# Taking the next tiles' output projection, norm and transposes ahead of each tile's gate projection in the conv stage

## What is computed

```python
yp = yp + concat(ya, yb) @ w_out            # layer 0: output projection and residual
h  = rmsnorm(yp, norm_w[1])
qkv, z, a, b = split(h @ w_in_c, C_SIZES)   # 2048 + 1024 + 8 + 8 columns
qkv, conv_new = causal_conv(qkv, prefix, conv_w)   # width 4, depthwise, then SiLU
# later, in the delta stage: o = rmsnorm(o, gdn_norm) * silu(z)
```

## Time and profile before

| | us |
|---|---|
| median of 3 timed runs | 4142.27 |
| lowest and highest of them | 4137.85, 4146.02 |
| profiled execution, span | 4139.1 |
| conv stage in it, first DMA to the last store's issue | 2158.5 to 3367.7 |
| its conv phases begin (group 0, 1, 2, 3) | 2339.98, 2616.00, 2892.43, 3204.17 |

### The profile page before, as it was taken

The page is one execution under the profiler, slowest core; times in us unless marked ns, Lnnn a source line. Parts: engine busy times, 40 slices in busy tenths (PEclk is TensorE's granted clock), DMA queues, the critical chain, the costliest instruction groups (busy, mean ns, idle before and its releaser), DMA issues. The chain is left out here.

```text
span 4139.1 us, 47583 instructions
## 1 busy us (share of the span) xinstructions
PE 3468.1 (84%) x15449; PEld 2016.0 (49%) x15449; DVE 1876.7 (45%) x3884; ACT 1383.0 (33%) x2827; POOL 858.9 (21%) x1709
## 2 busy tenths in 40 slices
PE   7999648999999897786367999989989956997998
PEld 4445324555555555563223444444444534665665
DVE  0000046677777877333810240431511546774674
ACT  1111126656666565640111111111111123442442
POOL 3112253222211110000000000000000006774672
PEclk9999868999999997787688999999989977997999
DMA  7334324544433330003314012011021032223321
GB/s 244 105 96 129 101 76 153 160 141 143 121 112 112 102 94 14 3 3 120 138 47 186 33 44 66 25 56 51 27 65 41 23 112 75 93 93 92 113 82 57
DMA packets 233111, 366.74 MB, mean 89 GB/s; under 512 B 45876, under 2 KB 130909, under 8 KB 228733
## 3 DMA queue, kind: packets, MB, share of 16 engines
q1 hardware_dynamic: 208064, 334.62, 25.2%
q10 hardware_dynamic: 20736, 21.05, 1.5%
q0 software_dynamic: 4096, 8.40, 0.8%
HBM read 279.22 MB, written 106.04 MB: 93 GB/s over the span
## 5 line engine op out<-in xcount | busy, mean ns | idle before, releaser
L1930 PE MATMUL QB<-hT,w_c 128*128 128x512 f32 x1024 | 449.4, 593 | 0.0
L328 PE MATMUL P0A<-w_all,hT 128*128 128x512 f32 (+1 forms) x1200 | 431.7, 521 | 0.0
L631 PE MATMUL PB<-wb,hT_ahead 128*128 128x512 f32 x704 | 366.1, 646 | 3.2 <-ACT prb L751 1.9
L655 PEld LDWEIGHTS PO<-vst,ptT 128*128 128x128 f32 x2176 | 295.4, 207 | 81.5 <-issue 43.6
L655 PE MATMUL PO<-vst,ptT 128*128 128x64 f32 x2176 | 308.7, 287 | 13.4 <-ACT ptT L771 13.2
L328 PEld LDWEIGHTS P0A<-w_all,hT 128*128 128x128 f32 x1200 | 207.5, 191 | 219.6 <-issue 219.6
L1930 PEld LDWEIGHTS QB<-hT,w_c 128*128 128x128 f32 x1024 | 190.0, 190 | 217.1 <-issue 217.1
L1875 PE MATMUL QS<-w_o,yT 128*128 128x512 f32 x544 | 274.6, 669 | 17.4 <-ACT yT L2043 17.4
L642 PE MATMUL PT<-ident,sm 128*128 128x128 f32 x1088 | 198.8, 308 | 106.0 <-ACT sm L763 105.8
L1899 PE MATMUL QA<-w_c,hT 128*128 128x512 f32 (+1 forms) x768 | 254.8, 488 | 5.7 <-ACT hT L2059 5.7
L771 ACT COPY ptT<-PT 128x512 f32<-128x512 f32 (+3 forms) x320 | 164.9, 518 | 275.1 <-PE PT L642 274.1
(11 more groups left out here) (412 smaller groups left out, 5317.7 us busy)
## 6 DMA issues: line engine op xcount, KB each, us to landing
wb<-in_w_in_ab SPq DMA_DIRECT2D x176, 512.0 KB, 3.7
out_c_all<-crow SPq DMA_DIRECT2D x256, 64.0 KB, 1.6
w_all<-in_w_in_ab SPq DMA_DIRECT2D x48, 256.0 KB, 8.1
out_pr_all<-pr_out SPq DMA_DIRECT2D x17, 546.0 KB, 2.9
pra<-out_pr_all SPq DMA_DIRECT2D x16, 546.0 KB, 4.6
x_rows<-in_x_all SPq DMA_DIRECT2D x17, 512.0 KB, 5.5
yab<-out_yab_all SPq DMA_DIRECT2D x17, 512.0 KB, 3.6
xin<-in_x_all SPq DMA_DIRECT2D x17, 512.0 KB, 4.2
```

The source lines that it names most:

```text
L328: ins = pe.matmul(PA[u % 6][:, 0:b - a], hT[:, t % (LAG + 2), c, :], w_all[:, c, a:b], start=(c == 0), stop=(c == KD - 1))
L631: ins = pe.matmul(PB[:, :], hT[:, 2 * q + k, :], wb[:, u % 4, k, :], start=(q == 0 and k == 0), stop=(q == 3 and k == 1))
L655: ins = pe.matmul(PO[:, h * HD:(h + 1) * HD], ptT[:, v % 2, k * P:(k + 1) * P], vst[:, 4 * c + k, a * HD:(a + 1) * HD], start=(c == 0 and ...
L1930: ins = pe.matmul(PB[b % 2][:, 0:N], w_c[:, c, b * P:(b + 1) * P], hT[:, c, 0:N], start=(c == 0), stop=(c == KD - 1))
```

## The change

On all engines the steps of a tile are put in another order, and the work runs further ahead. Ahead of `z_proj(T)` now stand, as one piece `ahead(T)`: `turn_h(T)`, the matmuls of `out_proj(T+1)`, and the transposes of `yab` for tile T+2 (`turn_y(T+2)`). `turn_h` writes to the banks `PB`, which hold nothing outside the conv blocks, in place of `PT`. ACT's `sub_front` is split into `turned_y` (the copies to `yT`) and `normed`; its order becomes `sub_back(T)`, `normed(T+1)`, `turned_y(T+2)`, then the gate's tanh of T. At the end of each of the first three groups the piece for the next group's first tile is run too: on PE between the matmuls of block 15 and the transposes of block 14, on the others behind the blocks. SP's loads and stores are cut and ordered to match. The first pieces stand in front of the loop, and in the last group (5 tiles) `left` shortens them. No arithmetic and no transfer is added or removed.

```diff
 sync:
+            def rows_in(T):
+                sp.wait_ge(S["yT_ps"], after(2 * T))
+                sp.dma_start(yab[:, :], io["yab_all"][ds(T * P, P), :]).then_inc(S["yab2_loaded"], 16)
+
+            def x_in(T):
+                sp.wait_ge(S["y1_ready"], after(2 * T))
+                sp.dma_start(xin[:, :], io["x_all"][ds(T * P, P), :]).then_inc(S["x2_loaded"], 16)
...
+            def ahead(T, left):
+                if left >= 1:
+                    sub_out(T + 1)
+                if left >= 2:
+                    x_in(T + 2)
+                if left >= 3:
+                    rows_in(T + 3)
+
             def group(G, n):
-                for s in range(n + 1):
-                    if s < n:
-                        if s < GT:
-                            next_in(G * GT + s)
-                        sub_out(G * GT + s)
+                for s in range(n):
+                    T = G * GT + s
                     if s:
-                        z_out(G * GT + s - 1)
+                        ahead(T, n - 1 - s if n > GT else 3)
+                    z_out(T)
                 blocks(G, n > GT)
+                if n == GT:
+                    ahead(G * GT + GT, 3)
 tensor:
-            def out_proj(T):
-
+            def turn_y(T):
                 pe.wait_ge(S["yab2_loaded"], after(16 * (T + 1)))
-                pe.wait_ge(S["hT2_sb"], after(2 * T))
+                pe.wait_ge(S["yT_sb"], after(2 * T))
...
+            def out_proj(T):
                 pe.wait_ge(S["yT_sb"], after(2 * T + 2))
                 pe.wait_ge(S["y1_ready"], after(2 * T))
...
             def turn_h(T, s):
                 pe.wait_ge(S["hn2_ready"], after(T + 1))
-                pe.wait_ge(S["yT_sb"], after(2 * T + 2))
+                pe.wait_ge(S["hT2_sb"], after(2 * T))
...
-                        ins = pe.transpose(PT[u][:, k * P:(k + 1) * P], hn[:, c * P:(c + 1) * P], ident[:, :])
+                        ins = pe.transpose(PB[u][:, k * P:(k + 1) * P], hn[:, c * P:(c + 1) * P], ident[:, :])
...
-            def z_proj(T, s):
+            def z_proj(T, s, G):
                 pe.wait_ge(S["hT2_sb"], after(2 * T + 2))
+                if s == 0:
+                    pe.wait_ge(S["crow_ready"], after(G * NBLK))
...
+                    if b == NBLK and not sample:
+                        pe.wait_ge(S["raw_ready"], after((G + 1) * NBLK))
+                        ahead(G * GT + GT, 0, 3)
...
+            def ahead(T, s, left):
+
+                turn_h(T, s)
+                if left >= 1:
+                    out_proj(T + 1)
+                if left >= 2:
+                    turn_y(T + 2)
+
             def group(G, n):
-                for s in range(n + 1):
+                for s in range(n):
                     T = G * GT + s
-                    if s < n:
-                        out_proj(T)
                     if s:
-                        z_proj(T - 1, s - 1)
-                    if s < n:
-                        if s == 0:
-                            pe.wait_ge(S["crow_ready"], after(G * NBLK))
-                        turn_h(T, s)
+                        ahead(T, s, n - 1 - s if n > GT else 3)
+                    z_proj(T, s, G)
                 blocks(G, n)
...
+            turn_y(0)
+            out_proj(0)
+            turn_y(1)
+            ahead(0, 0, 3)
             with pe.Fori(0, GROUPS - 1) as G:
 scalar:
+            def ahead(T, s, left):
+
+                sub_back(T, s)
+                if left >= 1:
+                    normed(T + 1)
+                if left >= 2:
+                    turned_y(T + 2)
...
                     if s:
-                        z_gate(T - 1, G)
-                    if s < n:
-                        sub_back(T, s)
+                        ahead(T, s, n - 1 - s if n > GT else 3)
+                    z_gate(T, G)
                 blocks(G, n)
...
+                if n == GT:
+                    ahead(G * GT + GT, 0, 3)
 vector:
             def group(G, n):
-                for s in range(n + 1):
-                    if s < n:
-                        residual(G * GT + s)
-                    if s:
-                        z_gate(G * GT + s - 1)
+                for s in range(n):
+                    T = G * GT + s
+                    if s and (n == GT or s < n - 1):
+                        residual(T + 1)
+                    z_gate(T)
                 blocks(G, n)
+                if n == GT:
+                    residual(G * GT + GT + 1)
```

More of the change, by code:

```diff
@@ L1833, in blocks @@
                           .then_inc(S["s_stored%d" % (b % 2)], 16)
-            def group(G, n):
-                for s in range(n + 1):
-                    if s < n:
-                        if s < GT:
-                            next_in(G * GT + s)
-                        sub_out(G * GT + s)
+            def ahead(T, left):
[5 more added lines that the diff above has]
+                    rows_in(T + 3)
+            def group(G, n):
+                for s in range(n):
+                    T = G * GT + s
                     if s:
-                        z_out(G * GT + s - 1)
+                        ahead(T, n - 1 - s if n > GT else 3)
+                    z_out(T)
                 blocks(G, n > GT)
+                if n == GT:
+                    ahead(G * GT + GT, 3)
             sp.dma_start(crw[0:DB * 3, :], io["state_conv"]).then_inc(S["pre_loaded"], 16)
+            rows_in(1)
+            sub_out(0)
+            x_in(1)
+            rows_in(2)
+            ahead(0, 3)
             with sp.Fori(0, GROUPS - 1) as G:
@@ L2027, in tanh_and_rows, with turned_y @@
                 act.activation(cvt[:, 0:N], cva[:, b % 2, 0:N], ACT.Tanh).then_inc(S["cvt_ready"], 1)
+            def ahead(T, s, left):
[4 more added lines that the diff above has]
+                    turned_y(T + 2)
             def group(G, n):
[L2030 removed]
+                for s in range(n):
                     T = G * GT + s
[L2032 to L2033 removed]
                     if s:
[L2035 to L2037 removed]
+                        ahead(T, s, n - 1 - s if n > GT else 3)
+                    z_gate(T, G)
                 blocks(G, n)
[L2040 removed]
+                if n == GT:
+                    ahead(G * GT + GT, 0, 3)
+            def turned_y(T):
                 for u in range(2):
@@ L2044, in sub_front, with normed @@
                        .then_inc(S["yT_sb"], 1)
+            def normed(T):
                 act.wait_ge(S["y1_ready"], after(2 * T + 2))
@@ L2058, in sub_back @@
                         h = hT[:, c, s * P:(s + 1) * P] if s < GT else hT_s[:, c, :]
-                        ins = act.activation(h, PT[u][:, k * P:(k + 1) * P], ACT.Copy, scale=nw1[:, c:c + 1])
+                        ins = act.activation(h, PB[u][:, k * P:(k + 1) * P], ACT.Copy, scale=nw1[:, c:c + 1])
                     ins.then_inc(S["hT2_sb"], 1)
@@ L2068, in _ @@
             act.wait_ge(S["c2_loaded"], after(16 * 4))
+            turned_y(0)
+            normed(0)
+            turned_y(1)
+            ahead(0, 0, 3)
             with act.Fori(0, GROUPS - 1) as G:
@@ L2201, in _ @@
             dve.wait_ge(S["pre_ready"], after(1))
+            residual(0)
+            residual(1)
             with dve.Fori(0, GROUPS - 1) as G:
```

## The result

The changed kernel takes 4017.16 us in the median of 4 runs (4012.09 to 4030.71), against 4140.06 for the kernel before in its 4 runs (4133.15 to 4146.02). The ratio is 0.9708, 95% interval 0.9688 to 0.9727: 123 us less. The forecast of 4026 was 9 us too high, and the time lies inside the stated range.

What follows compares the result with a forecast made beforehand. PE bounds the conv stage, with some 35 us a group lost to waits and slow clock. Gains of 3.5 + 31.9 + 32.3 + 48.8 = 116.5 us from 4142.3 gave 4026 us, range 4015 to 4046 (likeliest case 4019 to 4038).

Steps and rivals of the forecast that it cites:

- The tile in the loop: Middle of a group: a tile costs PE 30.9 us at full clock with no wait, against 37.06 in the old timeline.
- The waits of 1.82, 0.73, 4.69 and 4.29 us: PE's old waits for ACT's scalings, yT copies, block 14's chain and the group's first norm; all forecast to go.
- rival 3: Each tile keeps a new wait like the 0.73 us plus 1.8 of clock: 4066 us, or 4046 half as often; chance 0.10.
- The first conv phase: Stage's start: the first conv phase begins at 2336.5 instead of 2339.98, 3.5 us gained.
- The cycle: Conv phase to conv phase in a four-tile group: 240.7 + 0.4 + 1.2 + 1.8 = 244.1 us, against 276.02 and 276.43.
- the last one: Last group, five tiles: 262.9 us to the last conv phase against 311.74, 48.8 us gained.
- The covers named for ACT: In the gate projection, ACT's norm and yT copies finish before tanh is wanted, with about 2 us of slack.
- rival 4: xin landing later than 23 us after issue stops PE each tile; slower than before at 35 us, 4227 us; chance 0.02.
- The clock at the group ends: Slow clock in the first gate projection after each of three group ends: 1.8 us each, between 0 and 3.3.
- The sample tile's gate projection: Last group, turn_h(16) to z_proj(16): the one wait that stays, 1.9 us, with 1.4 us of slow clock.
- The idle time at a group's end: PE idles 0.4 us behind block 15 and 1.2 us for DVE's last copies before the gate projection.
- The doubt that the prediction raised over gathered transposes: Transposes gathered between wide matmuls might lower the clock at each tile: 23 to 43 us back, 4049 to 4069; chance 0.09.

Runs made afterwards that it cites:

- order_shared_bank: Changed kernel with turn_h back in the banks PT and the waits this needs, without the wait for raw at a group's end; 4022.0 us.
- early_start: Changed kernel with tile 0's yab transposes and output projection before the conv state's transposes, and ACT and DVE reordered to match; 3999.4 us.
- copies_first: Kernel before with turn_h in the banks PB and, inside groups, ACT's copies of the next tile to yT ahead of this tile's scalings; 4099.2 us.
- end_first: Changed kernel with the piece ahead() at a group's end put behind the transposes of blocks 14 and 15 on PE; 4043.6 us.
- transposes_x4: Changed kernel with the eight transposes of yab made four times over at each tile; 4049.7 us.
- bank_only: Kernel before with only turn_h moved to the banks PB and PE's two waits adapted, all streams in the old order; 4111.2 us.

## Why the prediction was right

The steps held one by one. The tile in the loop was forecast at 30.9 us and took 30.95. The waits of 1.82, 0.73, 4.69 and 4.29 us went, and none took their place: rival 3 has no row. The first conv phase was forecast at 2336.5 and began at 2336.22. The cycle was forecast at 244.1 and took 242.6; the last one at 262.9 and took 260.1. The covers named for ACT had the slack given, and `xin` landed 4.4 us after its issue by the page, far from the 23 us of rival 4.

Three terms were sized wrong, all on the safe side:

- *The clock at the group ends.* The prediction took 1.8 us for each of three, from the rows behind 1.90 us of idle. Measured was 15.69 - 15.59 = 0.1 behind 1.13 us. This is 5 us of the 9 by which the forecast missed. The bound of 0 was named, and is what came.
- *The sample tile's gate projection.* 1.4 us of clock were taken; this profile shows 0.1, and others 1.8 (order_shared_bank, early_start, copies_first) and 3.1 (end_first) behind the same wait of 1.82 or 1.83 us. PE's stream around that place is the same in all of them, so this looks like a matter of the execution and not of the kernel; with one profile of each kernel that is not shown.
- *The idle time at a group's end.* 0.4 + 1.2 forecast, 0.24 + 1.13 measured.

At the stage's start two errors cancelled: `out_proj(1)` began at 2213.19 and not at 2211.0, since the first projection began 1.6 us later than in the profile before (2191.19 against 2189.62) and ran 1 us longer, but `out_proj(1)` itself ran at full clock, 13.84 us instead of 16.4. In the profiles the forecast is missed by 5.9 us (a span of 4016.7 against 4022.6): the three terms above are 7 us too dear, and the rest took some 1.2 us more than the sum. The other 3 us are between the profiled span and the median of the runs, which lay 3.2 apart before and 0.5 after.

One reading in the prediction is off by a little: the losses behind the double waits inside the groups are 1.5 to 3.2 us in the trace and not 1.8 to 3.3. It moves the bounds of the rivals a little and not the forecast. The doubt that the prediction raised over gathered transposes is answered by transposes_x4: they cost no clock.

The changed kernel, then, gains in four steps, each shown by a kernel of its own, in us of the stage: banks of `turn_h` 29.1; ACT's copies ahead of its scalings 17.1; the rest of the running ahead inside groups 23.5; and across groups 54.6, of which 22.8 depend on the place of the last piece ahead of the transposes of blocks 14 and 15 (3 of them being that profile's sample tile). Since order_shared_bank shows the banks to be worth nothing in the new order, this is one path of steps and not a sum of independent parts.

What the prediction did not say is how much of the gain is clock: some 54 us, by the groups by line, against 65 of idle time.

## What to carry to other kernels

When TensorE bounds a stage, price each of its waits with the slow clock behind it: here 2 to 3 us of wait cost some 2 us more in the matmuls that follow, and two waits of 1.82 and 0.73 us with transposes between them cost more than one of 1.91. Put independent work of the next tiles between a producer and its consumer on PE before looking for more buffers; bank sharing cost 29 us in one order and nothing in the other. Look at a stage's first wide matmul too: what keeps it back may be a load or a queue that only later work needs.

## What the runs showed of the hardware

- A clock once raised was kept through 3.49 us of transposes alone (granted clock 1.00, transposes_x4), and through a single idle time of 0.73 us (copies_first) or 1.13 us (changed kernel): 0.1 us lost.
- Transposes alone raised the clock from 0.50 to 1.00 at the start of the stage (transposes_x4), and the matmuls behind them ran at full clock from the first.
- Behind one wait of 1.8 to 2.1 us the loss was 0.1 us at some places and 1.5 to 3.2 at others, also within one program (bank_only: 0.1 and 1.8 in turn). A wait of 3.36 us before `turn_h(0)` cost 0.1 in the changed kernel; in end_first, whose stream on PE is the same up to there, the same 3.36 us cost 1.3 in the output projection and 0.4 in the transposes before it. So the length of an idle time alone doesn't tell whether the clock falls. What does is left open; no run here was made to find it.
- Where it fell behind a single wait, the loss in the matmuls behind it was 1.3 to 3.2 us and did not grow with the idle time: 2.1 a place behind 2.7 us on the average, 1.9 behind 4.7.
